# Entry to the second feed-forward layer by halves and pairs of blocks, a buffer for the modulation rows, and shorter gate, score and local products

## What is computed

```
sh1, sc1, g1, sh2, sc2, g2 = split(silu(c) @ w_mod[i] + b_mod[i])          # six modulation rows per layer
x = layer_norm(ALPHA * x + g2 * swiglu(modulate(x, sh2, sc2)), ...)          # end of layer 0
hx = modulate(x, sh1, sc1)                                                   # layer 1
y = multiscale_pool(hx, pool_w, pool_scale)
x = layer_norm(ALPHA * x + g1 * y, ln_g[1, 0], ln_b[1, 0])
x = layer_norm(ALPHA * x + g2 * swiglu(modulate(x, sh2, sc2)), ...)          # swiglu(h) = (silu(h Wg) * (h Wu)) Wo
...
z = (g_lr @ gla_gate_w2) + gla_gate_b;  log_a = log_sigmoid(z) / 16          # g_lr: 16 columns of h @ w_in
b = cumsum(log_a) in chunks of 64;  a = where(causal, qd kd^T, 0) inside each chunk of 64
sc = q k^T * scale - slope * |distance|, causal over 256 rows;  softmax      # MoBA, 8 heads
```

## Time and profile before

| | before |
|---|---|
| median of 3 runs | 1162.19 us (1161.38 to 1164.38) |
| the profiled execution's own time | 1161.04 us |
| its span | 1159.3 us |
| TensorE busy | 1125.7 us, 97% |
| VectorE busy | 768.2 us, 66% |
| ScalarE busy | 567.1 us, 49% |
| mean granted TensorE clock | 0.99 of full speed |

### The profile page before, as it was taken

One profiled execution on the slowest core, in us unless ns is written; L12 is line 12 of the kernel. 1 busy time (PEld: TensorE's weight loads), 2 busy tenths in 40 slices (PEclk: granted clock), 3 DMA queues, 4 the chain that ended last, 5 costly groups with the idle time before them and its releaser, 6 DMA issues.

```text
span 1159.3 us, 15345 instructions
## 1 busy us (share of the span) xinstructions
PE 1125.7 (97%) x6322; PEld 949.2 (82%) x6322; DVE 768.2 (66%) x877; ACT 567.1 (49%) x779; POOL 61.9 (5%) x119
## 2 busy tenths in 40 slices
PE   5999999999999988999999999999999999999998
PEld 3787766889998767999988877886888889998886
DVE  1697498888696899875543955455657667664444
ACT  2642367564344224644442767554855365553342
POOL 0011130001110201000000000010000000000000
PEclk8999999999999998999999999999999999999999
DMA  9986560779897974685554797776724446555540
GB/s 328 381 280 238 196 184 14 263 245 307 305 338 242 334 262 162 219 284 165 183 189 128 174 234 166 161 157 134 182 110 145 145 146 224 186 183 196 193 154 37
DMA packets 120391, 236.80 MB, mean 204 GB/s; under 512 B 5633, under 2 KB 61250, under 8 KB 120194
## 3 DMA queue, kind: packets, MB, share of 16 engines
q1 hardware_dynamic: 105984, 185.48, 52.5%
q0 software_dynamic: 14048, 50.09, 12.3%
q10 hardware_dynamic: 290, 0.26, 0.1%
HBM read 234.75 MB, written 1.05 MB: 203 GB/s over the span
## 4 chain that ended last, share of the span: by engine, by line
PE 85%; DVE 7%; DMA 3%; SPq 2%; issue 2%; ACT 1%; DVEq 0%; ACTq 0%
PE ps L1848 17%; PE ps L1849 17%; PE ps L1850 17%; PE ps L1891 8%; PE ps L1890 8%; PE ps L1889 8%; PE ps L1988 2%; DVE wL L1054 1%; PE ps L2110 1%; PE ps L2149 1%; DMA mod<-in_w_mod 1%; DVE g2b L1138 1%; DMA modraw<-in_w_mod 1%; PE ps L2038 1%; SPq L419 1%
## 5 line engine op out<-in xcount | busy, mean ns | idle before, releaser
L1054 DVE TENSOR_TENSOR wL<-raw,wH 128x1024 fp32r<-128x1024 f32 x328 | 397.0, 1221 | 237.9 <-ACT wH L590 236.6
L590 ACT ACTIVATE wH<-raw 128x1024 fp32r<-128x1024 f32 x328 | 342.7, 1058 | 388.0 <-PE ps L1850 237.2
L1848 PE MATMUL ps<-wH,aH 128*128 128x512 f32 (+1 forms) x592 | 236.1, 399 | 9.2 <-DVE aL L1066 3.4
L1849 PE MATMUL ps<-wL,aH 128*128 128x512 f32 (+1 forms) x592 | 230.8, 390 | 0.0
L1850 PE MATMUL ps<-wH,aL 128*128 128x512 f32 (+1 forms) x592 | 230.8, 390 | 0.0
L1889 PE MATMUL ps<-aH,wH 128*128 128x256 f32 x768 | 219.4, 286 | 0.0
L1891 PE MATMUL ps<-aH,wL 128*128 128x256 f32 x768 | 217.3, 283 | 0.0
L1890 PE MATMUL ps<-aL,wH 128*128 128x256 f32 x768 | 217.3, 283 | 0.0
L1889 PEld LDWEIGHTS ps<-aH,wH 128*128 128x128 f32 x768 | 147.4, 192 | 1.0 <-issue 0.7
L1890 PEld LDWEIGHTS ps<-aL,wH 128*128 128x128 f32 x768 | 147.4, 192 | 1.0 <-issue 1.0
L1891 PEld LDWEIGHTS ps<-aH,wL 128*128 128x128 f32 x768 | 147.4, 192 | 0.0
(11 more groups left out here) (309 smaller groups left out, 1255.0 us busy)
## 6 DMA issues: line engine op xcount, KB each, us to landing
raw<-in_ffn_w_in SPq DMA_DIRECT2D x88, 512.0 KB
modraw<-in_w_mod POOLq DMA_DIRECT2D x80, 512.0 KB, 6.4
raw<-in_w_in SPq DMA_DIRECT2D x32, 1024.0 KB
raw<-in_ffn_w_out SPq DMA_DIRECT2D x22, 1024.0 KB
raw<-in_w_up SPq DMA_DIRECT2D x16, 1024.0 KB
raw<-in_w_down SPq DMA_DIRECT2D x16, 1024.0 KB
mod<-in_w_mod SPq DMA_DIRECT2D x8, 1024.0 KB, 11.8
raw<-in_attn_w_qkv SPq DMA_DIRECT2D x8, 1024.0 KB
```

The source lines that it names most:

```text
L590: nc.scalar.activation(wH[:, n % WS, :], raw[:, (n // 2) % RAW, (n % 2) * 1024:(n % 2) * 1024 + 1024], ACT.Copy).then_inc(w_hi, 1)
L1054: V.tensor_tensor(wL[:, n % WL, :], raw[:, (n // 2) % RAW, (n % 2) * 1024:(n % 2) * 1024 + 1024], wH[:, n % WS, :].bitcast(fp32), ALU.subt ...
L1848: T.matmul(outp, xh, h, start=first, stop=False)
L1849: T.matmul(outp, xh, l, start=False, stop=False)
```

## The change

It has five parts.

1. The totals of rows 3 to 7 get a place of their own, `psb`, so that the tile after them can be loaded at once. The pool scale, which lived in `psb` from early on, is now loaded by POOL after row 7 is summed. DVE does three more steps in `in0` (chunks 3, 5 and 7) and none in `out0` after sub 11. PE sums rows 3 to 6 after chunks 3, 5, 7 and 10, and row 7 after sub 6 of `out0`. The products that prepare the rows of layer 1 move up as well.
2. At the entry `affine(0, 1)`, `affine(1, 0)` and the scale columns (`lncol_of`) move ahead of `pooled(0)`.
3. `hat` of the first 128 rows is done in two halves, and ACT and DVE split the transposed blocks in pairs (`hi_x3`, `low_x3`) between single subs.
4. The 16-column product takes high and low part of the weights as 32 columns: 16 products where there were 24. The sums of log_a are split into high and low parts (on ACT and DVE), and the two running sums are 8 products in the split format where there were 4 float32 ones. The local products are 16 of 64 by 64 where there were 8 of 128 by 128.
5. MoBA leaves out the keys 128 to 255 of the first 128 rows, which the causal mask removes: one of the two score products of a head has 128 columns, and the following steps on DVE and ACT shrink to 384 columns.

```diff
+LRP = 2 * GRANK
+VEC_IN = 16 * (LRP // GRANK + 1)
+MKEYS = (slice(0, P), slice(P, 3 * P))
-FF0_SELECT = {3: 3, 6: 4, 8: 5}
-FF0_PUT = {4: 3, 7: 4, 9: 5}
+FF0_SELECT = {3: 3, 5: 4, 7: 5, 10: 6}
+FF0_PUT = {4: 3, 6: 4, 8: 5}
+ROW_PSB = range(3, 8)
...
         def vec_row(v):
+            if v in ROW_PSB:
+                return psb[:, :]
             if v < IN_FF0 - 1:
...
-                        if k == MT - 1 and v <= IN_FF0 - 1:
+                        if k == MT - 1 and v <= IN_FF0 - 1 and v - 1 not in ROW_PSB:
                             pool.wait_ge(vec_sum, v)
...
+                    if n == KT * (IN_FF0 - 1) + 4:
+                        pool.wait_ge(vec_sum, ROW_PSB[-1] + 1)
+                        pool.dma_start(psb[:, :], a["pool_scale"].to_broadcast([P, D])).then_inc(pscale_in, 16)
...
+            def hi_x3(j):
+                g = GROUPS["x3"] + j
+                act.wait_ge(t_done, g + 1)
+                for q in range(2):
+                    k0 = 4 * j + 2 * q
+                    tmp = tf[:, g % 2, 2 * q * P:2 * q * P + 2 * P].rearrange("p (k s) -> p k s", k=2)
+                    src = tbank(g)[:, 2 * q * P:2 * q * P + 2 * P].rearrange("p (k s) -> p k s", k=2)
+                    for k in range(2):
+                        ins = nc.scalar.activation(tmp[:, k, :], src[:, k, :], ACT.Identity,
+                                                   bias=lncol[:, 1, 1, k0 + k:k0 + k + 1], scale=lncol[:, 1, 0, k0 + k:k0 + k + 1])
+                    link(ins)
+                    nc.scalar.activation(aH[:, k0:k0 + 2, 0:P], tmp, ACT.Copy).then_inc(x3_hi if q == 0 else t_hi, 1)
...
+                        if k == KT - 1 and n // KT - 1 in ROW_PSB and n // KT in ROW_PSB:
+                            dve.wait_ge(vec_sum, n // KT)
...
+                affine(0, 1)
                 for j in range(4):
                     low(j)
                 vec_put(IN_FF0 - 1)
-                affine(0, 1)
+                dve.wait_ge(mod_out, NMOD0 + IN_FF0)
+                lncol_of(1).then_inc(lncol_ready, 1)
+                dve.wait_ge(pool_h, 3)
+                affine(1, 0)
                 dve.wait_ge(ln_x, TT + 1)
                 pooled(0)
                 spread(0)
                 rstd(2, 0)
-                hat(0)
-                dve.wait_ge(mod_out, NMOD0 + IN_FF0)
-                lncol_of(1).then_inc(lncol_ready, 1)
-                for j in range(2, 4):
-                    adv(first + j)
-                dve.wait_ge(pool_h, 3)
-                affine(1, 0)
-                lo_t("x3", 0, norm=1)
+                hat(0, halves[0], hat_half)
+                hat(0, halves[1], ln_hat)
+                for j in range(2):
+                    for q in range(2):
+                        adv(first + 2 + 2 * j + q)
+                        low_x3(j, q)
                 affine(1, 1)
-                lo_t("x3", 1, norm=1)
-                for j in range(4, 6):
-                    adv(first + j)
...
+                        if j == 2 and c in (3, 5, 7):
+                            vec_steps(1)
...
+                        if k < 12:
+                            vec_steps(1)
+                        elif k == 12:
+                            dve.wait_ge(pscale_in, 16)
+                            link(V.tensor_tensor(g1b[:, :], g1b[:, :], psb[:, :], ALU.mult))
+                            gated(0)
                 if layer == 0:
-                    vec_put(7)
-                    vec_steps(1)
...
+                    gated(1)
...
-                    if layer == 0 and k in (5, 12):
-                        vec_total({5: 6, 12: 7}[k])
+                    if layer == 0 and k == 6:
+                        vec_total(7)
...
-                    for k in range(KT):
-                        ins = three(ps[0:GRANK, 6, 0:S], lrH[:, k, :], lrL[:, k, :], aH[:, k, :], aL[:, k, :],
-                                    k == 0, k == KT - 1)
+                    for i, act_ in enumerate((aH, aL)):
+                        for k in range(KT):
+                            ins = T.matmul(ps[0:LRP, 6, 0:S], lrw2[:, k, :, :].rearrange("p l r -> p (l r)"),
+                                           act_[:, k, :], start=i == 0 and k == 0, stop=i == 1 and k == KT - 1)
...
-                            ins = T.matmul(side(1 - j)[:, t, :], cst[:, tab:tab + P], la[:, t, :], start=True, stop=True)
+                            for i, part_ in enumerate((laH, laL)):
+                                ins = T.matmul(side(1 - j)[:, t, :], tabr[:, j * P:(j + 1) * P], part_[:, t, :],
+                                               start=i == 0, stop=i == 1)
...
-                            ins = T.matmul(tbank(g)[:, h * P:(h + 1) * P], qkT[:, 1, h, t * P:(t + 1) * P],
-                                           qkT[:, 0, h, t * P:(t + 1) * P], start=True, stop=True)
+                            for half in range(2):
+                                r0, c0 = GCH * half, t * P + GCH * half
+                                ins = T.matmul(tbank(g)[r0:r0 + GCH, h * P + r0:h * P + r0 + GCH],
+                                               qkT[:, 1, h, c0:c0 + GCH], qkT[:, 0, h, c0:c0 + GCH], start=True, stop=True)
...
-                for t in range(TT):
-                    ins = T.matmul(ps[:, 6 + h % 2, t * S:(t + 1) * S], mT[:, h, t * P:(t + 1) * P], mT[:, 8 + h, :],
+                for t, keys in enumerate(MKEYS):
+                    ins = T.matmul(ps[:, 6 + h % 2, keys], mT[:, h, t * P:(t + 1) * P], mT[:, 8 + h, 0:(t + 1) * P],
                                    start=True, stop=True)
```

More of the change, by code:

```diff
@@ L1509, in ln_pool @@
                 rstd(2, 1)
-                hat(1)
+                hat(1, full, ln_hat)
                 for j in range(7, 10):
@@ L1580, in swiglu @@
[L1580 to L1591 removed]
+                        elif k == 8:
+                            vec_put(7)
@@ L2379, in mtranspose @@
                     pe.wait_ge(m_Tc, h)
[L2380 to L2381 removed]
+                for j in range(3):
+                    ins = T.transpose(ps[:, 4, j * P:(j + 1) * P], pe_[:, h % 2, j * P:(j + 1) * P], ident)
                 ins.then_inc(m_T, 1)
```

150 lines of the change are left out of this document (93 added, 57 removed).

## The result

The changed kernel takes 1149.04 us (median of 5 runs, 1148.33 to 1150.33), the kernel before 1162.09 us (5 runs, 1161.38 to 1164.38). The ratio is 0.9889, with a 95% interval of 0.9875 to 0.9902. It is faster by 13 us, where 9.6 were forecast. The profiled execution took 1149.76 us, 11.3 less than that of before (1161.04).

The account below looks back on a forecast made before the run. TensorE was taken to bound nearly all of the kernel, VectorE's list the entry. Gains of 2.8 + 3.7 + 3.1 = 9.6 us took the median from 1162.19 to 1152.6 us, 8-in-10 range 1149 to 1157.5.

Parts of the forecast that it names:

- Term 1: Rows' sums up to the end of out0: two small TensorE stops and the low clock behind one go, 2.8 us.
- The case in which a sum by itself lowers the clock: Row sums on TensorE around out0: if one alone lowers the clock, the gain there is 1.3 us, not 2.8.
- Term 2: Entry, from the end of out0 to rows 128 to 255: VectorE on time and new order gain 3.7 us.
- Term 3: Less TensorE work in the 16-column product, running sums and scores, less a loss in local products: 3.1 us gained.
- A: Memory: in0's three extra tiles delay weights, so ScalarE's adv and chunk 10's silu come late; 1156.2 us, chance 0.13.
- B: VectorE stays late at the end of out0 from new waits for tiles; 1158.4 us, chance 0.07.
- C: Row 7's sum, at sub 6 of out0, stops TensorE because a tile is 12 us late; 1166.5 us, chance 0.02.
- D: Clock stays up or later advs hide its loss, and small products are cheap; 1150.6 us and below, chance 0.08.

Follow-up runs that it names:

- wide local products: Changed kernel with only the local products put back to 8 of 128 by 128; 1149.68 us (4 runs).
- part 1 alone: Kernel before with only the rows' own buffer and the new places of steps and sums, old entry and products; 1154.07 us, ratio 0.9936.
- parts 4 and 5 alone: Kernel before with only the new products: 32-column product, split running sums, small local products, shorter scores; 1155.74 us, ratio 0.9953.
- old entry: Changed kernel with the entry back in its old order: affine in its old places, hat whole, blocks by fours; 1147.82 us, ratio 0.9887 to the kernel before.
- parts 2 and 3 alone: Kernel before with only the new entry: affine and scale columns moved ahead, hat by halves, pairs of blocks; 1163.17 us, ratio 1.0010.
- by half: Changed kernel with the 32 local records reordered: all heads' first halves, then all second halves, where it alternated; 1150.86 us (2 runs).
- again: Changed kernel timed once more without any edit; 1149.98 us (4 runs).

## Why the prediction was right, and where it was wrong

**Term 1** (2.8 us forecast) measured 2.80 in the two profiled executions. The nine further traces with part 1 have E nearer to the start by another 0.3 to 0.6 us: from the first product behind the attention to E they took 221.8 to 222.1 us, where the changed kernel's first trace has 222.4 and before 225.2. The pieces are as named: no stop for the hidden block in most traces (0.26 us in the first), none before the sum of row 7, and a full clock behind it. The case in which a sum by itself lowers the clock did not come: the sum stands at 379.93 with the clock at 1.00. The three traces with the old rows (before and the kernels with parts 2 and 3, or 4 and 5, alone) have the stop (0.61, 1.55, 0.75 us) and 3.4 us at the lower level behind it; none of the ten with the new rows has either.

**Term 2** (3.7) measured 4.07, and its places came as worked out: second window products at E + 4.2 (4.2), first product of `in1` at E + 17.6 (17.6), low parts 1.47 us apart (1.5), `pooled(1)` at E + 23.1 (23.4), fifth sub at E + 27.2 (27.5), rows 128 to 255 at E + 35.25 (35.6). The stop was 2.46 us and not 4, because the first subs ran at 1.2 GHz, which I had not foreseen and which cost only idle time. With wide local products they ran at the full clock, and there the stop was 3.57. The low clock behind the stop took 4.45 - 2.72 = 1.7 us from 12 products, at the upper end of the 0 to 1.8 that I gave, and a net 0.9 when it was taken away, the value I used.

What the prediction had wrong here is whose the gain is. I wrote it under "Parts 2 and 3". The 4.07 us are those by which VectorE was late at E, and part 1 removes that. The list of VectorE up to `hat` of rows 128 to 255 is as long in the new order as in the old (that `hat` ends at E + 28.0 in the changed kernel and at E + 28.3 with part 1 alone). The new order lets TensorE begin 1 to 2 us sooner, work it can't use, and puts the stop and its low clock where TensorE has no time to spare. What the order costs shows when all traces with either order are counted from the transposes of rows 0 to 127:

| kernels | these transposes | from them to rows 128 to 255 |
|---|---|---|
| old order, old rows (before; parts 4 and 5 alone) | E + 19.7, 19.6 | 19.6, 19.65 us |
| old order, new rows (part 1 alone; old entry) | E + 15.0, 14.0 | 19.6, 19.65 us |
| new order, old rows (parts 2 and 3 alone) | E + 19.6 | 21.4 us |
| new order, new rows (changed, by half, again; wide) | E + 15.0 in all four | 20.3, 20.3, 20.3; 21.5 us |

Behind the transposes the new order costs 0.7 us in the three traces with 3.4 us of low clock there, and 1.7 to 1.9 in the two with 6.8. Ahead of them it gains nothing: they stand at E + 15.0 whether the second window products run at the lower level or not, and in the old order at E + 14.0 in the one trace in which these run at the full clock. So the new order costs 0.7 to 1.9 us behind the transposes, and up to 1 us ahead of them. The medians (1.2 us lost on the kernel before, 1.2 in the changed one) are in keeping with that, but too coarse to show it.

**Term 3** (3.1, between 2.0 and 4.2) measured 5.05, outside its bounds, and this is the step that failed. Three of its entries hold: the 16-column product 0.93 (0.9), the running sums 1.58 (1.6), the scores 1.80 (1.7). The local products were booked as a loss of 1.1 us, "0.75 lost" for 32 records at 0.08 and 0.35 for "two such changes" of width, and they gained 0.72: 0.034 a record, and 0.08 for the changes. I had bounded the record from below by half of 0.111, "nothing lost", as if the cost could fall only with the moving columns or only with the weight columns. Both fell by half, and the cost fell from 0.118 us to 0.034, less than a third. The pair 0.63 against 0.43 us from which I took 0.2 for a change of width holds another cost, which no run here names. Why half the columns on both sides cost less than half is not shown; the order of the output halves accounts for 0.012 us of a record.

By the 62 ns a small product that I weighed, as an estimate, the 32 records would take 2.0 us; the trace says 1.08. The section of the Trainium skill that I cited for it (TensorE: Matmul & The Clock Gate, Back-to-back issue gap) gives these 62 ns only with hardware decode off, and an issue floor of some 25 ns otherwise, which 0.034 us does not contradict. And of the Trainium skill's TensorEngine Tiling (Array Packing), Key Properties, I took only that a change of mode drains, where the trace has 0.08 us, and left out the next property, that tiles can run in parallel.

**Sum and median.** 9.6 forecast, 11.3 between the two profiled executions: +0.4 from term 2, +1.95 from term 3, -0.65 from a late start. The rest to 13 us is that I counted both kernels' medians as equally far from their profiled executions. That I count as chance, and so the -0.65: the first product behind the attention, where the trace is 0.65 us late, lies between 200.7 and 202.6 us in the traces of this case.

**The rivals.** A (memory) did not come: ScalarE's silu waits for TensorE, though the DMA share rose from 0.93 to 0.99, which leaves little room for more loads there. B (VectorE late): it waits 4.21 us for TensorE at the first `residual`. C: the sum of row 7 has no stop. D was partly so: small products cheap, later `adv`s hiding about half of the low clock. By its number the result is D's: 1149.04 lies under its 1150.6, to which I gave 0.08, and not in the forecast's own 1150.5 to 1155, to which I gave 0.70. What put it there is term 3 and the two medians, not a clock that stayed up.

One sentence ahead of the prediction is not exact: a transpose shows one record a block and not two (8 for 8 blocks at 438.83). No term used it.

## What to carry to other kernels

When an engine is late at a stage, ask first what made it late, and price the cure of that before any new order inside the stage: with VectorE on time the old order was at least as good. An earlier first product is worth nothing if the same list of work feeds the sixth; count the feeding engine's list up to the last piece that the stage can't do without, and prefer one stop ahead of a run of products to one in its middle. Before moving a step ahead of a wait, look for the next condition of the same instruction (here the accumulators that `pooled(1)` reads), since a trace names only the last. And before two traces are compared, see whether the clock fell over the same products in both, and count from a point behind the place where it did not.

The lowest median here is that of the changed kernel with the fifth sub's `adv` first, 1147.58 us; four other kernels lie within 0.7 us of it, which these runs can't tell apart, but its trace is also the shortest from E to rows 128 to 255. In it the `adv`s of the last two subs of the first eight end at E + 31.5 and rows 128 to 255 start at E + 33.5, so little is left without taking work from VectorE.

## What the runs showed of the hardware

- In all six traces with a stop of TensorE of 2.3 to 3.6 us behind the fourth sub, products at 1.2 GHz (0.63 us for 0.39) follow within 1 us of its end. In the one trace with 2.35 us of needless transposes in the stop the clock stayed at 2.4 GHz.
- The length of a stop alone doesn't tell it. Behind 1.63 us the clock stayed full; behind the same 1.50 us before the first product of `in1` it was low in five traces and full in three; behind 0.61 us in `out0` of the kernel before it was low.
- The same program meets the low level at other products from one execution to the next. Of the four traces with the changed kernel's entry three had 3.4 us of it behind the stop, with rows 128 to 255 at E + 35.3, and one 6.8, with E + 36.5. The kernels of E + 33.5 and E + 34.4 with the fifth sub's `adv` first differ in it too. So do the traces with part 1 alone and with the old entry, over the second window products, and it moves the transposes behind them by 1.0 us in the old order.
- 64-column products against 64 columns of weights took 0.034 us each when neighbours wrote different halves of the output rows, 0.046 when they wrote the same, and 0.118 at 128 by 128.
